# Opening in column halves, and four pairs of expert places loaded as two transfers each

## What is computed

```python
h = rms_norm(x) * (1 + scale1(c)) + shift1(c)      # scale1, shift1: silu(c) @ w_ada, per group
[u_pool | v_conv] = h @ w_in                       # 1536 columns: 512 pool, 512 a, 512 g
a = pooling mixer(u_pool);  b = conv module(a_half * sigmoid(g_half))   # depthwise conv, width 31
m = sigmoid(h Wg_a) * a + sigmoid(h Wg_b) * b
x = x + gate1(c) * (m @ w_out)
h2 = rms_norm(x) * (1 + scale2(c)) + shift2(c)
x = x + gate2(c) * moe(h2)                         # 32 experts, top 4, clamped SwiGLU
y = rms_norm(x)
```

## Time and profile before

| what | us |
|---|---|
| median of the three runs shown | 1157.67 |
| lowest, highest | 1156.29, 1159.33 |
| profiled execution, device time | 1158.99 |
| its span, first to last instruction | 1157.1 |
| TensorE busy in it | 1128.9 |
| VectorE busy in it | 500.3 |

### The profile page before, as it was taken

One profiled execution on the slowest core, in us unless ns is written; L12 is line 12 of the kernel. 1 busy time (PEld: TensorE's weight loads), 2 busy tenths in 40 slices (PEclk: granted clock), 3 DMA queues, 4 the chain that ended last, 5 costly groups with the idle time before them and its releaser, 6 DMA issues.

```text
span 1157.1 us, 16132 instructions
## 1 busy us (share of the span) xinstructions
PE 1128.9 (98%) x5964; PEld 459.7 (40%) x5965; DVE 500.3 (43%) x1143; ACT 177.5 (15%) x333; POOL 29.5 (3%) x78
## 2 busy tenths in 40 slices
PE   9999999999999999999999999999999999999996
PEld 6676675633333333333322333333333333333332
DVE  3398524654333443344333443344334433333334
ACT  2001301311111111111111112111111111111112
POOL 4002300000000000000000000000000000000000
PEclk9999999999999999999999999999999999999998
DMA  9977699699999999999999999999999999999994
GB/s 348 373 278 273 251 299 321 217 368 428 428 428 428 428 430 428 428 428 430 428 428 428 429 428 428 428 429 428 429 427 429 428 429 429 428 427 429 428 428 195
DMA packets 58012, 456.13 MB, mean 394 GB/s; under 512 B 7125, under 2 KB 26385, under 8 KB 31237
## 3 DMA queue, kind: packets, MB, share of 16 engines
q1 hardware_dynamic: 53872, 452.35, 94.4%
q10 hardware_dynamic: 4117, 3.47, 1.3%
HBM read 454.40 MB, written 1.40 MB: 394 GB/s over the span
## 4 chain that ended last, share of the span: by engine, by line
PE 78%; DMA 21%; DVE 1%; issue 0%; POOL 0%; DVEq 0%; SPq 0%; POOLq 0%
PE bank L1690 46%; DMA ring<-in_exp_w_up 7%; DMA ring<-in_exp_w_gate 7%; PE bank L1476 5%; PE bank L1423 4%; PE bank L1717 4%; PE bank L1642 4%; DMA arena<-in_exp_w_up 3%; DMA arena<-in_exp_w_gate 3%; PE bank L1563 2%; PE bank L1772 1%; PE bank L1546 1%; PE bank L1650 1%; PE bank L1397 1%; PE bank L1708 1%; PE bank L1320 1%
## 5 line engine op out<-in xcount | busy, mean ns | idle before, releaser
L1690 PE MATMUL bank<-ring,arena 128*64 128x512 f32 x2112 | 472.5, 598 | 11.3 <-DMA ring<-in_exp_w_gate 10.1
L1690 PEld LDWEIGHTS bank<-ring,arena 128*64 128x64 f32 x2112 | 146.9, 137 | 313.6 <-issue 286.5
L1690 PE MATMUL bank<-arena 128*64 128x512 f32 x1056 | 236.1, 595 | 5.3 <-DMA arena<-in_exp_w_gate 5.1
L1690 PEld LDWEIGHTS bank<-arena 128*64 128x64 f32 x1056 | 73.3, 137 | 155.5 <-issue 137.9
L780 ACT ACTIVATE arena<-arena 32x256 f32<-32x256 f32 x136 | 56.0, 412 | 422.8 <-DVE arena L1163 421.6
L1247 DVE TENSOR_SCALAR arena<-bank 128x512 f32<-128x512 f32 x33 | 22.8, 691 | 168.0 <-PE bank L1690 168.0
L1254 DVE TENSOR_SCALAR arena<-bank 128x512 f32<-128x512 f32 x33 | 22.8, 691 | 167.8 <-PE bank L1690 167.8
L1232 DVE TENSOR_TENSOR x<-x,bank 128x512 f32<-128x512 f32 x132 | 84.5, 681 | 13.0 <-PE bank L1717 13.0
L1269 DVE TENSOR_TENSOR arena<-bank,biases 128x512 f32<-128x512 f32 x66 | 42.5, 685 | 110.2 <-PE bank L1690 110.2
L793 ACT ACTIVATE arena<-arena 128x512 f32<-128x512 f32 x33 | 20.8, 629 | 356.7 <-DVE arena L1247 356.7
L1717 PE MATMUL bank<-arena 64*128 64x512 f32 x264 | 65.6, 615 | 0.0
(11 more groups left out here) (306 smaller groups left out, 742.8 us busy)
## 6 DMA issues: line engine op xcount, KB each, us to landing
ring<-in_exp_w_down SPq DMA_DIRECT2D x43, 2048.0 KB, 28.9
ring<-in_exp_w_up SPq DMA_DIRECT2D x43, 2048.0 KB, 28.8
ring<-in_exp_w_gate SPq DMA_DIRECT2D x42, 2048.0 KB, 28.1
arena<-in_exp_w_gate SPq DMA_DIRECT2D x22, 2048.0 KB, 26.4
arena<-in_exp_w_up SPq DMA_DIRECT2D x21, 2048.0 KB, 28.7
arena<-in_exp_w_down SPq DMA_DIRECT2D x20, 2048.0 KB, 30.3
ring<-in_w_ada SPq DMA_DIRECT2D x24, 1024.0 KB, 9.9
ring<-in_gate_w SPq DMA_DIRECT2D x8, 1024.0 KB, 7.8
```

Of the source, the lines that this page charges most:

```text
L1690: ins = mm(out[64 * hh:64 * hh + 64, :], lhs(k), w[:, D * (k % 2) + HALF * hh:D * (k % 2) + HALF * (hh + 1)], start=(done is y_mm and k == ...
```

## The change

Three parts.

*Opening.* A scale or shift piece is now four row blocks and one half of 512 columns, and a w_in piece four row blocks and 512 columns (one kind: g, a or pool). So scale1 comes in two column halves with a bias row, a `to_columns` and a ScalarE copy each; the first four w_in tiles are the four of g, their first half of rows computed ahead of the second half of scale1's effect. The a tiles come next with the shift in them. One token tile's square moves from ScalarE to VectorE, one tile's scaling and four of the eight copies of turned tokens from VectorE to ScalarE. `fill(3)`, 4, 6, 3 and 2 in the opening become `fill(12)` ahead of `turn_x`.

*What follows from it.* GLU and convolution begin with one tile alone (six taps), then the second alone, then both. The layer norm's mean and variance products move two gate tiles later (8 and 10).

*Experts.* The first three refills (pairs 9, 10, 11) and the last pair of all are two transfers of 1 MB, each released by the use of its own slot; the last product waits for the last pair by halves. In front of the first item one `fill` becomes two, and the last `fill(1)` becomes `fill(5)`.

```diff
-SPLIT = 4
+SPLIT, HALVED = 4, 3
-FRONT = ([("scale", 0, j) for j in range(4)] + [("in", c, 0) for c in (4, 2)]
-         + [("shift", 0, j) for j in range(4)] + [("in", c, 0) for c in (5, 3, 0, 1)]
+FRONT = ([("scale", 0, 0), ("scale", 0, 1), ("in", 2, 0), ("scale", 1, 0), ("scale", 1, 1), ("in", 2, 1)]
+         + [("shift", h, j) for h in range(2) for j in range(2)] + [("in", c, j) for c in (1, 0) for j in range(2)]
-MEAN_AT, VAR_AT, STATES_AT = 6, 8, 10
+MEAN_AT, VAR_AT, STATES_AT = 8, 10, 10
@@ SyncE
+            def refill_halves(e, q, before):
+                i, p = q % PER_EXPERT, q % PAIRS
+                w = (wg_v, wu_v, wd_v)[i // 2][e + q // PER_EXPERT]
+                at = sp.value_load(base_i[0:1, bass.ds(e + (before + 1), 1)], min_val=1, max_val=MAX_ITEMS)
+                for half in range(2):
+                    sp.wait_ge(piece_used, at * PIECES + (F_END - PIECES + 2 * ((q - PAIRS) % PER_EXPERT) + 1 + half))
+                    sp.dma_start(slots(2 * p + half, 1), w[:, i % 2, SLOT * half:SLOT * (half + 1)]) \
+                        .then_inc(slot_ld[2 * p + 1 - half], 16)
@@ ScalarE
+            for t in range(2):
+                a.activation(view(2304 + D * t, D), x[:, t, :], ACT.Square, accum_out=stat[:, t:t + 1]).then_inc(ssq, 1)
+            a.activation(h2[:, 1, :], x[:, 1, :], ACT.Copy, scale=stat[:, 5:6]).then_inc(xn_ready, 1)
+            for k in range(4, KD):
+                a.activation(hS[:, k, :], bank[k % 4][:, 0:TOK], ACT.Copy).then_inc(xT_act, 1)
@@ VectorE
+            glu((0,))
+            conv((0,), 0, ALONE)
+            glu((1,))
+            conv((1,), 0, ALONE)
+            conv((0, 1), ALONE, CONV_SPLIT)
@@ TensorE
-            first_rows(2)
-            fill(3)
+            first_rows(2, bank[4])
+            fill(12)
+            first_half("scale", 0, 0)
+            first_half("scale", 0, 1)
+            to_columns(0, 0)
+            for n in range(UNSHIFTED):
+                chunk(n, 0)
+                if n < 2:
+                    first_half("scale", 1, n)
+                elif n == 2:
+                    to_columns(0, 1)
+            first_rows(0, bank[4])
+            first_rows(1, bank[5])
+            for n in range(UNSHIFTED):
+                chunk(n, 1)
+                first_half("shift", n // 2, n % 2)
+                if n == 3:
+                    to_columns(1, 0)
+                    to_columns(1, 1)
@@ ahead of the first item
-            fill(1, bank[1])
+            fill(2, bank[1])
-            fill(1, bank[1])
+            fill(5, bank[1])
```

More of the change, by code:

```diff
@@ L233, in build @@
         cols_ld = sem("cols_ld")
-        cT1 = sem("cT1")
         c_cols_ready = sem("c_cols_ready")
@@ L495, in refill @@
                     load(e + q // PER_EXPERT, q)
[L497 to L500, removed]
+            def refill_halves(e, q, before):
[6 more added lines that the diff above has]
+                        .then_inc(slot_ld[2 * p + 1 - half], 16)
+            last_turn = E - E % TURN - TURN
+            for q in range(PAIRS, PAIRS + HALVED):
+                refill_halves(0, q, 0)
+            with sp.Fori(0, last_turn - TURN + 1, TURN) as e:
+                refill(e, range(PAIRS + HALVED, PAIRS + HALVED + TURN * PER_EXPERT))
+            last = (TURN + E % TURN) * PER_EXPERT - 1
+            refill(last_turn, range(PAIRS + HALVED, last))
+            refill_halves(last_turn, last, (last - PAIRS) // PER_EXPERT)
             at = sp.value_load(base_i[0:1, E - 1:E], min_val=E - 1, max_val=MAX_ITEMS)
@@ L1365, in _ @@
             pe.wait_ge(ada_ld, 16)
-            first_rows(2)
-            fill(3)
-            pe.wait_ge(cT_ready, 1)
-            fill(4)
-            first_half("scale", 0)
-            fill(6)
-            first_half("scale", 1)
+            first_rows(2, bank[4])
+            fill(12)
+            pe.wait_ge(xn_ready, TT)
+            for k in range(4):
+                turn_x(k)
             pe.wait_ge(c_cols_ready, 1)
@@ new lines, in _ @@
+            pe.wait_ge(shift_ready, 2)
+            for k in range(KD):
+                q = k % 4
+                ins = mm(bank[4][32 * q:32 * q + 32, :], shT[:, k, :], front_piece(piece_of[("in", 2, k // 4)])[1][:, k % 4, :],
+                         start=(k < 4), stop=(k >= 4), skip_group_check=True)
+            ins.then_inc(shift_mm, 1)
+            pe.wait_ge(cols_ready, 1)
+            pe.wait_ge(dw_ld, 16)
+            for c in range(CT):
+                ins = tr(bank[5][:, 32 * c:32 * c + WIDTH], dw_stage[:, P * c:P * (c + 1)], ident[0:WIDTH, 0:WIDTH])
+                if c == 0:
+                    ins.then_inc(piece_used, 8)
@@ L1467, in _ @@
+            for m in range(UNSHIFTED):
+                mm(bank[m][:, 0:TOK], rows[:, 2, P * m:P * (m + 1)], group_of, start=False, stop=True,
+                   skip_group_check=True).then_inc(in_mm, 1)
+            for n in range(UNSHIFTED, 12):
+                if n < 8:
+                    pe.wait_ge(sig_ready, n - 3)
+                else:
+                    pe.wait_ge(u_ready, n - 7)
+                chunk(n, 0)
+                chunk(n, 1).then_inc(in_mm, 1)
             for n in range(2 * KD):
@@ L1678, in gather_end, with product @@
                 gather_strips(lookup=True).then_inc(xg_mm, 1)
-            def product(out, lhs, g, j, c0, done, before_used=None):
+            def product(out, lhs, g, j, c0, done, before_used=None, last=False):
                 for k in range(KD):
@@ L1785, in expert @@
                 with pe.Fori(first_item, next_first) as n:
-                    item(n, g, j)
+                    item(n, g, j, last)
             with pe.Fori(0, E // TURN) as g:
```

311 lines of the change are left out of this document (138 added, 173 removed).

## The result

The changed kernel takes 1163.1 us in the median of ten runs (1160.2 to 1169.1), the kernel before 1157.7 in ten runs beside them (1154.3 to 1159.3). The ratio is 1.0053, with a 95% interval of 1.0041 to 1.0065: **slower by 6.1 us** (4.7 to 7.5), where 1157.8 had been forecast and 1161.5 was the upper end of the range. (The medians alone differ by 5.4 us.) The profiled execution took 1163.38 us with a span of 1161.5.

What follows compares the result with a forecast made beforehand. The DMA stream at 428 GB/s was taken to bound the kernel, becoming continuous after TensorE's front and the first refills. Opening +2.6, refills -2.3, last pair -0.2 make +0.1: 1157.8 us, range 1152.5 to 1161.5.

Steps and rivals of the forecast that it cites:

- When the opening starts: TensorE's first token turn: at 12.5 us, when the 24 fill instructions end, 3.3 us earlier than 15.81.
- How long the opening is: First turn to first w_in tile with shift: 34.8 us before, +5.9 added work; tile at 53.2, 2.6 us later.
- the open wait: Opening: 0.5 us, as the last to_columns and VectorE's shift copy no longer have half a tile to cover them.
- What the opening moves: Later loads, convolution, sum over channels and state stores: cost nothing; the sum's cover grows from 3.4 to 7 us.
- First refills: Experts' first refilled pairs: halves and fills gain 2.3 us, bounds 3.4 gained and 0.6 lost.
- The dry stretch: DMA engines near 236 to 238 us at 98 GB/s, awaiting the first refill; with the slow stretches after, 3.4 us lost.
- the list of losses: DMA shortfall against 428 GB/s around the first refills: 1.54, 0.97 and 0.86 us, 3.4 together.
- the whole 2.77 us: Item 0's product, 9.79 us against 7.02 elsewhere: by the skill's rule alone the added fills would give all this back.
- The last pair: Second down pair's weight load at the end: landing by halves removes a 0.28 us wait, -0.2, bounds 0 and -0.3.
- The first (the opening is really earlier): Opening: new order hides part of its added work and refills give their full 3.4; -5.1, 1152.6 us; chance 0.27.
- The second: Ahead of item 0: fills at half clock delay it 1.9 us; +3.0 to +4.5, 1160.7 to 1162.2 us; chance 0.2.
- The third: Halved transfers: each of four additional transfers opens a 2.9 us gap, 11.4 together, 1171.7 us; chance 0.02.

Runs made afterwards that it cites:

- the start alone: Kernel before with the norm spread over both engines, fill(12) ahead of the turning, first two scale pieces behind the first four turns; old column order: 1156.3 us, 0.9994.
- the run with added fills: Changed kernel with fill(20) ahead of the turning, one fill after each of the first six turns, four behind the last to_columns: 1164.3 us, 1.0049.
- the column halves alone: Changed kernel with the opening's start and the experts' part put back as in the kernel before; new pieces, tiles and column order stay: 1167.2 us, 1.0086.
- start and fills: Kernel before with the earlier start and two and five fills ahead of the first item, no halved transfers, old column order: 1156.5 us, 0.9987.
- start and experts' part together: Kernel before with the earlier start, halved refills, halved last pair and added fills ahead of the first item; old column order: 1155.2 us, 0.9975.
- the experts' part alone: Kernel before with three refilled pairs and the last pair in halves and the added fills ahead of the first item; old opening: 1155.7 us, 0.9985.
- the fills alone: Kernel before with two and five fills instead of one and one ahead of the first item, nothing else: 1155.3 us, 0.9975.
- the second form: Changed kernel with one fill after each of the first six turns only, fill(12) as it is: 1164.8 us, 1.0055.
- the opening without fills: Kernel before without the fills of its opening, only the first nine matrices ahead of everything staying: 1159.8 us, 1.0022.

## Why the prediction was wrong

By its own steps:

**When the opening starts.** Forecast 12.5, profiled 11.45. The norm was sized well (11.4), the fills were not: ten of the 24 instructions were priced at full clock and the rest as cold, which gives an end at 12.5; they ended at 9.7 in this profile, and at 13.5 in two others. So the forecast let the fills run up to the turning, and TensorE stood still there for 1.75 us. The worth of the start by the prediction's prices, less the two scale pieces, the transpose and the fills, is 3.3 - 1.9 - 0.2 + 0.6 = 1.8 us; the start alone measured 0.7 (between 1.9 gained and 0.6 lost), which neither confirms it nor rules it out.

**How long the opening is.** Forecast 40.7; 40.1 at full clock in the run with added fills, 41.6 by taking the cost of the slow groups off the changed kernel, 47.7 as it ran. The added work was sized well: the terms that belong to the column halves (two `to_columns` 1.6, bias rows 1.7, half tiles 0.7, the open wait 0.5) make 4.5 us, and 4.6 were measured at an unchanged start. A single bias row is 0.92 (two such rows: 1.83), as taken.

**The step that failed** is the silent one: every price was taken from the earlier trace rows at full clock, and the opening's clock was taken to stay there. In the changed kernel's profile the low spells cost 6.1 us. The four combinations show what start and column order cost together with it (both rows with the old experts' part):

| ratio to before | old column order | column halves |
|---|---|---|
| old start | 1 | 1.0086 |
| new start | 0.9994 | 1.0069 |

The halves cost some 9 to 10 us whatever the start, and only half of that is work. The mean granted clock of the runs bears it out: 0.995 on the average of the kernel before, 0.989 to 0.993 in the five of the column halves alone. A clock that is 0.005 lower over 1165 us is 5.8 us, an estimate from these means. Work and clock make 4.6 + 5.8 = 10.4 for the 9 to 10 measured.

For the changed kernel the same estimate is smaller than its one profile says. Its ten runs average 0.9940, the profiled one has 0.992; the two kernels with the old opening and the same fills at item 0 average 0.9973. The difference over 1163 us is 3.8 us. With the opening's 2.4 us at full clock (11.45 + 41.6 against 50.63; 2.6 had been forecast) and the 1.7 that the experts' part gives back, that is 4.5 us of the 5.4 to 6.1 measured; the rest isn't placed. Within the ten, the lowest and the highest clock go with the longest and the shortest times: 1169.1 us at 0.989, 1160.2 and 1160.8 at 0.997. The last two are still 3 us above the kernel before, so the clock isn't the whole of it.

Not all of the spells are the column order's. The first one, 12 to 20 us, follows the 1.75 us in which TensorE stood still, and the old order with the new start has it at the same place behind 1.47 us (start and fills). Across the fourteen profiles: in six TensorE stood still once for 1.33 to 2.56 us ahead of the turning, and all six have a low spell after that; in the other eight its longest stand there was 0 to 0.88 us, and three have a spell, at 20 to 28 us (the two of the column halves with the old start, and start and experts' part together). That is an order of events, one profile each, and no proof; but the prediction had no term for either, though the earlier trace rows had shown what the clock does to TensorE. It used that only at item 0, where the fall was already in the trace.

**What the opening moves.** Cost nothing, as forecast: cover 7.9 us, and from the fifth tile to item 0 the delay changes from 8.5 to 9.0.

**First refills.** The gain in the profiles is 4.6 us, forecast 2.3, bound 3.4; by the ratio of the experts' part alone it is 1.7 (0.8 to 2.8). The bound was made for a clock that stays up, as it did, and was still too low. Summed in stretches of 4 us over the 60 us from the issue of pair 8, the engines fall short of 428 GB/s by 4.5 us in the kernel before, not 3.4, since the list of losses ended at 250 us and the earlier trace rows is followed by ten more at 401 GB/s; in the changed kernel it is 1.4, with the fills alone 2.2. That makes 3.1 us; the other 1.5 of the 4.6 is spread over 840 us that read 427 to 430 GB/s, and can't be placed. The mechanism was half right. The dry stretch was the loss, but its cause was the slow first item, and the added fills mend most of it alone (0.9975). The halves, which the prediction put first, add nothing that the times show.

The Trainium skill, "TensorE: Matmul & The Clock Gate", section on why this matters, advises to leave no long idle gaps between matmul bursts, and by it the prediction had computed the whole 2.77 us for the fills: at item 0 the traces agree in what the fills bring (9.79 us to 7.09), though in three of seven profiles the fall came ahead of the pause. In the opening the six stands of 1.33 us and more, each with a low spell later, agree with it in kind too. But it doesn't cover all: in the column halves alone the clock fell to 0.50 with TensorE busy 2.00 us of 2 in each stretch from 4 us on, and the six fills of the second form left it at 0.50 from 14 to 18 us.

**The last pair.** Forecast -0.2, measured nothing: the tail is 26.9 us in both. The step misread its row. In the kernel before, thirteen other groups of weight loads of that product show the same pause of 0.28 or 0.29 us, ended by "issue", and so it is in the changed kernel:

```profile
1142.31 0.14 PEld L1717 LDWEIGHTS bank<-ring,arena 128*64 128x64 f32 x2 [0.29 <-issue]
1142.74 0.14 PEld L1717 LDWEIGHTS bank<-ring,arena 128*64 128x64 f32 x2 [0.28 <-issue]
```

The 0.28 us of the earlier trace rows were that ordinary pause, put down to the DMA because one landed in it.

**The rivals.** The first (the opening is really earlier) fell with the fifth tile. The second named the right sign and nearly the right time, for a wrong reason: the fills ahead of item 0 don't stand in the way, they gain 2.9 us. The third fell: no stretch behind a halved refill is empty. The result came by a fourth case that wasn't listed.

**Open.** What makes the clock fall in the column order was not found: neither fills at its thin places nor the old start mends it. Of the profiles with column halves all six have a low spell between 8 and 28 us, and two of them (the changed kernel and the second form of fills) one more from 52 us on; of the four with the old order, old start and its fills none has; of the three with the old order and the new start two have. A kernel that differs from the changed one in the stand ahead of the turning alone was not run, so the share of start and order in the changed kernel's loss is an estimate. One profile of each kernel and the clock means of its runs are what there is.

## What to carry to other kernels

Price a reordering of TensorE's work at both clock levels: a stretch of short products, transposes and waits that ran at full clock in one order may not in another, and in a sum made at full clock the half-clock time (here 6 us in the profile, some 4 in the mean of the runs) was the largest term missing. Ask of every earlier start whether it leaves the engine standing. Where a trace shows TensorE at half clock in a product that releases a transfer, a few cheap matmuls ahead of it are worth trying by themselves and first; here two changed numbers gave 2.9 us, more than all the rest, and that kernel (1155.3) beats both the one before and the changed one. Cutting a column range in two doubles every per-piece step (bias row, column turn, copy, wait), and these lay on the bound engine.

## What was not expected of the hardware

The granted clock reads 1.00 in the first microseconds although TensorE runs at half speed there. In the kernel before, fourteen fill instructions took 3.23 us and twelve a little later 1.53, 0.23 and 0.13 us each; in the opening with the earlier start 24 took 5.42 us up to 13.5 us; the same opening in start and fills, and the changed kernel, took 2.94 for them, from 6.9 and 6.8 us on. When the full rate comes differs between executions that have the same instructions up to there, by some 7 us. The Trainium skill, "TensorE: Matmul & The Clock Gate", section on the HAM clock gate, says that the throttled state is the default, which activity ends, and that the point is run-variable; these rows agree. So the fills ahead of the turning are worth less, or cost more, than their full-clock price, and one profile of an opening is a sample, not a value.

One kernel's time can go with its mean granted clock over 9 us: the opening without fills took 1154.9 us at 0.996 and 1164.2 at 0.984. A median of few runs of such a kernel says little.
